# Three empty buffers in SBUF: the normed stream, the second operand and the arena start 192 bytes further on against the weights

## The chip, the cores and the metric

The kernel runs on one core of a Trainium2 chip. The metric is the device time of one execution in microseconds (us); the median of three runs before the change is 3683.33 us.

## The reference

The model is two stacks of two layers each over 512 tokens of width 1024, in float32. The first stack also carries 256 context tokens. Every layer is a mixer and a feed-forward part:

```
first stack, layer 0:  mLSTM heads and a 31-tap convolution      h @ w_in ... @ w_out
first stack, layer 1:  attention with 16 heads, 96 wide          h @ w_in, @ w_uq, @ w_ukv ... @ w_out
first stack, each:     x + gate * ((gelu(conv3(g)) * val) @ ffn_w_out),   g, val = h @ ffn_w_in
second stack, each:    z = h @ w_in;  differential attention and three dilated windows
                       merged = gate0 * (oa @ w_a) + gate1 * (ob @ w_b);  x + rms(merged @ w_out)
                       x + rms((silu(g) * u) @ w_down),                   g, u = h @ w_gate_up
h is always a normed (and in the first stack modulated) x
```

Most of the arithmetic is a dense product of a 1024-wide stream with a weight matrix.

## The kernel before

Tokens lie on the free axis and features on the 128 partitions, so a product is computed as weights (stationary, 128x128 blocks) against the stream (moving, 512 columns for the latent tokens and 256 for the context tokens), gathered in a PSUM bank. The weights come from one stream in HBM, in chunks of eight 128x128 blocks. SyncE loads a chunk into `w_raw`, ScalarE rounds it into `w_hi` (line 333), GpSimd writes the rest `w_raw - w_hi` into `w_lo` (line 3542), and TensorE multiplies when both are there. Three such places rotate.

Every float32 product is made of three fp32r matmuls, with both operands split in a high and a low part (lines 283 to 290):

```
for k, ((lh, ll), (rh, rl)) in enumerate(pairs):
    pe.matmul(dst, lh, rh, start=(begin and k == 0), stop=False)
    pe.matmul(dst, lh, rl, start=False, stop=False)
    last = pe.matmul(dst, ll, rh, ...)
```

The profile names the moving operand first and the stationary one second: `pB<-h_lo,w_hi` streams `h_lo` past a block of `w_hi`. TensorE's order is written out by hand; each matmul has its own weight load.

Moving operands are: `h_hi`, `h_lo` (the normed stream, 512 columns a block), `b_hi`, `b_lo` (the second operand: the activations that go into an output matrix), `xh_*` and `xb_*` (the same for the context tokens, 256 columns, in the arena), and, in a part of the feed-forward layers of the second stack, seven half-size products for a pair of chunks (lines 1090 to 1092, 256 columns, 12 matmuls each; Strassen's scheme). These seven take their moving operands, in this order, from `h`; from `xc_t`; from `attP_t` and `attT_t`; from `h`; from `attT_t` for two blocks and `combo_rest`, `attA_t` for two; from `h`; and from `hsum_t`, `arena_t`, `arena_u`. Their weights are halves of `w_hi`, `w_lo` and the pair `w_hi6`, `w_lo6`. In the attention of the second stack the projections of the next heads (line 2840, 512 columns) are put between the small matmuls of scores, transposes and weighted sums. `HOLD` matmuls (line 392) multiply a constant by the identity where TensorE would otherwise have nothing to do.

**Places in the row.** Tensors lie one behind the other in each partition's row, in the order of the program, each start rounded up to 32 bytes. In bytes: `x` 16384, `xc` 8192, `h_hi`, `h_lo`, `b_hi`, `b_lo` 16384 each, `w_raw` 16384, `w_hi` and `w_lo` 12288 each, `w_hi6`, `w_lo6`, `combo_rest` 2048 each, `pc` 1956 (to 1984), `cm` 3584, `mod` 768, `attA`, `attP`, `attT` 6144 each, `hsum` 3072, then 3904 of small tensors, then the arena (53200). Counted modulo 1024 from where `x` starts:

- `xc_t`, `h_*`, `b_*`, `w_raw`, `w_hi`, `w_lo`, `w_hi6`, `w_lo6`, `combo_rest`: remainder 0, as all sizes up to there are whole multiples of 1024
- `attA_t`, `attP_t`, `attT_t`, `hsum_t`: remainder 192, since 1984 + 3584 + 768 = 6336 = 6 x 1024 + 192
- the arena with `xh_*`, `xb_*`, `arena_t`, `arena_u`: remainder 0 again, since 192 + 3904 = 4096

Blocks inside a tensor start at multiples of 512 bytes (stationary) and 1024 or 2048 bytes (moving).

Of the kernel before, what the change touches and what calls it, by code (L numbers as in the profile page):

```python
# [21 lines left out]
P = 128  # L22
# [115 lines left out]
def program(nc, stream, ada, xT, cT, cond, lam, pcol, cmat, trope, brope, bmask, out):  # L138
    with ExitStack() as ctx:
        def sb(name, shape, dt=F32):  # L140
            return ctx.enter_context(nc.sbuf_tensor(name, shape, dt))
# [7 lines left out]
            pass  # L149
        xc = sb("xc", [P, KD, C])  # L150

        with nc.sbuf_tensor("under", [P, 4, KD * T], F32) as under:
            pass
        h_hi, h_lo = sb("h_hi", [P, KD * T], F32R), sb("h_lo", [P, KD * T], F32R)
        b_hi, b_lo = sb("b_hi", [P, KD * T], F32R), sb("b_lo", [P, KD * T], F32R)
        w_raw = sb("w_raw", [P, SLOTS + 1, KD * P])
        w_hi, w_lo = sb("w_hi", [P, SLOTS, KD * P], F32R), sb("w_lo", [P, SLOTS, KD * P], F32R)
        w_hi6, w_lo6 = sb("w_hi6", [P, HALF_K], F32R), sb("w_lo6", [P, HALF_K], F32R)
# [11 lines left out]
        cond_sb = sb("cond_sb", [P, 2 * KD])  # L170
        cond_pad = sb("cond_pad", [P, KD, 32])
        lam_junk = sb("lam_junk", [P, 64])
        with nc.sbuf_tensor("arena", [P, ARENA], F32) as arena:
            pass
        with nc.sbuf_tensor("mla_under", [P, 5376], F32), nc.sbuf_tensor("mla_q", [P, 4, T], F32R) as mla_q, nc.sbuf_tensor("mla_k", [P, 4, TC], F32R) as mla_k:
# [3753 lines left out]
```

## Time and profile before

| what | before |
|---|---|
| median of 3 runs | 3683.33 us (3680.15 to 3687.66) |
| the profiled execution | 3687.39 us, its span 3685.5 us |
| TensorE matmul busy | 3575.2 us (97%), 21374 matmuls |
| VectorE / ScalarE / GpSimd busy | 54% / 44% / 36% |
| granted TensorE clock, mean | 0.993 |
| DMA | 335.87 MB, mean 91 GB/s |

The span is the time from the first to the last instruction of the profiled execution; its own time is 1.9 us longer. The end of a matmul is modelled and overlaps the next one's start, so the pace of TensorE is read from start to start, and a busy share of 97% does not say that the matmuls follow one another as fast as they could.

### The profile page before, as it was taken

How to read it: one execution, taken by the hardware profiler on the slowest of the kernel's cores; microseconds unless marked ns; L12 is line 12 of the kernel's file. 1: busy time of each engine (PE TensorE's matmuls, PEld its weight loads, DVE VectorE, ACT ScalarE, POOL GpSimd, SP SyncE). 2: the span in 40 equal slices, each digit the busy share in tenths (PEclk: the TensorE clock that was granted, in tenths of full speed). 3: DMA queues.
4: the chain of work that ended last, by engine and by line, in shares of the span. 5: the costliest groups of instructions: out<-in, count | busy, mean ns of one | idle time of the engine just before them, and what ended most of it. 6: DMA issues, size and time to landing. Idle time of an engine off the chain costs nothing.

```text
span 3685.5 us, 56698 instructions
## 1 busy us (share of the span) xinstructions
PE 3575.2 (97%) x21374; PEld 2943.5 (80%) x21374; DVE 1996.1 (54%) x3030; ACT 1627.2 (44%) x2837; POOL 1326.6 (36%) x618
## 2 busy tenths in 40 slices
PE   7999999999999999999999999999999999999998
PEld 5875788888877777888777778789977777878997
DVE  4757553333357775343555553657556565356555
ACT  4344432221266663232655542545455554335444
POOL 2530332232331113444422234345542333434555
PEclk9999999999999999999999999999999999999999
DMA  5368321111220002322311222222322222222332
GB/s 210 118 210 306 106 77 63 63 63 63 69 80 24 24 24 92 103 92 97 102 58 63 70 75 97 73 100 87 115 89 71 65 70 69 86 92 75 109 103 92
DMA packets 85384, 335.87 MB, mean 91 GB/s; under 512 B 9648, under 2 KB 9776, under 8 KB 78640
## 3 DMA queue, kind: packets, MB, share of 16 engines
q1 hardware_dynamic: 84448, 330.79, 27.0%
q8 instruction: 147, 2.41, 0.3%
q10 hardware_dynamic: 720, 2.10, 0.2%
q14 instruction: 69, 0.57, 0.1%
HBM read 329.18 MB, written 2.10 MB: 90 GB/s over the span
## 4 chain that ended last, share of the span: by engine, by line
issue 45%; PE 37%; POOL 14%; DVE 3%; ACT 1%; POOLq 0%; ACTq 0%; DVEq 0%
POOL w_lo L3542 14%; PE pB L287 6%; PE pB L288 6%; PE pB L289 6%; PE pT L1090 2%; PE pT L1091 2%; PE pT L1092 2%; PE pT L289 1%; PE pT L288 1%; PE pT L287 1%; PE pO L287 1%; PE pO L1090 1%; PE pO L1092 1%; PE pO L1091 1%; PE pO L288 1%
## 5 line engine op out<-in xcount | busy, mean ns | idle before, releaser
L3542 POOL TENSOR_TENSOR w_lo<-w_raw,w_hi 128x1024 fp32r<-128x1024 f32 x448 | 1095.7, 2448 | 2075.2 <-ACT w_hi L333 2074.1
L333 ACT ACTIVATE w_hi<-w_raw 128x1024 fp32r<-128x1024 f32 x448 | 472.3, 1055 | 568.2 <-PE pB L289 372.6
L287 PE MATMUL pB<-h_hi,w_hi 128*128 128x512 f32 x1508 | 594.8, 394 | 18.6 <-DVE h_lo L477 6.0
L288 PE MATMUL pB<-h_lo,w_hi 128*128 128x512 f32 x1508 | 587.4, 390 | 0.0
L289 PE MATMUL pB<-h_hi,w_lo 128*128 128x512 f32 x1508 | 586.9, 389 | 0.0
L287 PE MATMUL pB<-b_hi,w_hi 128*128 128x512 f32 (+1 forms) x1084 | 400.9, 370 | 7.9 <-POOL w_lo L3542 4.3
L288 PE MATMUL pB<-b_lo,w_hi 128*128 128x512 f32 (+1 forms) x1084 | 396.0, 365 | 0.0
L289 PE MATMUL pB<-b_hi,w_lo 128*128 128x512 f32 (+1 forms) x1084 | 395.6, 365 | 0.0
L287 PEld LDWEIGHTS pB<-h_hi,w_hi 128*128 128x128 f32 x1508 | 283.7, 188 | 93.2 <-issue 15.5
L289 PEld LDWEIGHTS pB<-h_hi,w_lo 128*128 128x128 f32 x1508 | 283.5, 188 | 59.6
L2840 PE MATMUL pB<-h_hi,w_hi 128*128 128x512 f32 x800 | 330.4, 413 | 0.0
L288 PEld LDWEIGHTS pB<-h_lo,w_hi 128*128 128x128 f32 x1508 | 283.8, 188 | 56.6 <-issue 1.2
L2840 PE MATMUL pB<-h_hi,w_lo 128*128 128x512 f32 x800 | 314.6, 393 | 0.0
L2840 PE MATMUL pB<-h_lo,w_hi 128*128 128x512 f32 x800 | 314.0, 393 | 0.0
L1116 POOL TENSOR_TENSOR w_lo<-w_raw,w_hi 128x512 fp32r<-128x512 f32 x144 | 206.6, 1449 | 180.9 <-ACT w_hi L1111 177.1
L287 PEld LDWEIGHTS pB<-b_hi,w_hi 128*128 128x128 f32 x1084 | 205.1, 189 | 45.6 <-POOL w_lo L3542 4.7
L289 PEld LDWEIGHTS pB<-b_hi,w_lo 128*128 128x128 f32 x1084 | 205.2, 189 | 33.1
L288 PEld LDWEIGHTS pB<-b_lo,w_hi 128*128 128x128 f32 x1084 | 205.4, 189 | 32.3 <-issue 1.2
L2840 PEld LDWEIGHTS pB<-h_hi,w_hi 128*128 128x128 f32 x800 | 150.4, 188 | 53.9 <-issue 24.9
L2840 PEld LDWEIGHTS pB<-h_hi,w_lo 128*128 128x128 f32 x800 | 150.3, 188 | 33.6
L2840 PEld LDWEIGHTS pB<-h_lo,w_hi 128*128 128x128 f32 x800 | 150.9, 189 | 31.2 <-issue 5.1
L3051 ACT ACTIVATE attT<-pT 128x256 f32<-128x256 f32 (+1 forms) x64 | 31.5, 492 | 223.5 <-PE pT L2898 223.5
(673 smaller groups left out, 7200.5 us busy)
## 6 DMA issues: line engine op xcount, KB each, us to landing
w_raw<-stream SPq DMA_DIRECT2D x520, 512.0 KB, 3.3
under<-ada SPq DMA_DIRECT2D x42, 1024.0 KB, 5.3
arena<-ada SPq DMA_DIRECT2D x6, 1024.0 KB, 16.8
x<-xT SPq DMA_DIRECT2D x1, 2048.0 KB, 8.1
out<-x SPq DMA_DIRECT2D x8, 256.0 KB, 2.1
xc<-cT SPq DMA_DIRECT2D x1, 1024.0 KB, 26.5
arena<-bmask ACTq DMA_DIRECT2D x1, 1024.0 KB, 4.9
w_hi<-arena SPq DMA_DIRECT2D x4, 192.0 KB, 9.9
```

Of the source, the lines that this page charges most:

```text
L287: pe.matmul(dst, lh, rh, start=(begin and k == 0), stop=False)
L288: pe.matmul(dst, lh, rl, start=False, stop=False)
L289: last = pe.matmul(dst, ll, rh, start=False, stop=(end and k == len(pairs) - 1))
L333: act.activation(w_hi[:, s, :], w_raw[:, s, :], ACT.Copy).then_inc(hi_ready, 1)
L1090: pe.matmul(dst, wh[:, o], hh, start=begin, stop=False, skip_group_check=True)
L1091: pe.matmul(dst, wh[:, o], hl, start=False, stop=False, skip_group_check=True)
L1092: last = pe.matmul(dst, wl[:, o], hh, start=False, stop=(kt == 3), skip_group_check=True)
L1116: pool.tensor_tensor(lo, block_source(n, i), hi.bitcast(F32), ALU.subtract).then_inc(block_lo, 1)
L2840: last = pe.matmul(bank[s][:, :], wl if i % 3 == 2 else wh, hl if i % 3 == 1 else hh, start=(i == 0), stop=(i == CHUNK - 1))
L3051: act.activation(flat(attT)[:, o:o + w], pT[:, 0:w], ACT.Copy).then_inc(pair_ca, 1)
L3542: pool.tensor_tensor(w_lo[:, s, :], w_raw[:, s, :], w_hi[:, s, :].bitcast(F32), ALU.subtract).then_inc(lo_ready, 1)
```

## The change

Three buffers that nothing reads or writes are allocated. The first (192 bytes) stands in front of `h_hi`, the second (832 bytes) behind `b_lo`, the third (192 bytes) in front of the arena. `under`, which names the room of `h` and `b` under another type, and all the names laid over the arena start behind the buffers too. No instruction is added, removed or reordered.

```diff
@@ -149,10 +149,12 @@
         xc = sb("xc", [P, KD, C])
 
+        sb("place_h", [P, 48])
         with nc.sbuf_tensor("under", [P, 4, KD * T], F32) as under:
             pass
         h_hi, h_lo = sb("h_hi", [P, KD * T], F32R), sb("h_lo", [P, KD * T], F32R)
         b_hi, b_lo = sb("b_hi", [P, KD * T], F32R), sb("b_lo", [P, KD * T], F32R)
+        sb("place_w", [P, 208])
         w_raw = sb("w_raw", [P, SLOTS + 1, KD * P])
@@ -170,6 +172,7 @@
         lam_junk = sb("lam_junk", [P, 64])
+        sb("place_arena", [P, 48])
         with nc.sbuf_tensor("arena", [P, ARENA], F32) as arena:
             pass
```

Modulo 1024, `h_*` and `b_*` go from 0 to 192, and so does the arena (1024 + 192 bytes further on). Everything from `w_raw` to the small tensors moves by 192 + 832 = 1024 bytes and keeps its remainder: the weights, `combo_rest` 0, the `att` strips and `hsum` 192. `x` and `xc` do not move.

## Rows read from the trace of the kernel before

**Rows 1.** The page, busy time and granted clock in 40 slices

```profile
PE 3575.2 (97%) x21374; PEld 2943.5 (80%) x21374; DVE 1996.1 (54%) x3030; ACT 1627.2 (44%) x2837; POOL 1326.6 (36%) x618
...
PEclk9999999999999999999999999999999999999999
```

**Rows 2.** Waits of TensorE, longest: us in total, times, longest

```profile
PE pS L491 <- ACT attT L356: 17.0, 1, 17.0
```

**Rows 3.** Timeline of TensorE, feed-forward chunks: start, length

```profile
1500.24 0.39 PE L287 MATMUL pB<-h_hi,w_hi 128*128 128x512 f32 x1
...
1505.68 0.39 PE L287 MATMUL pB<-h_hi,w_hi 128*128 128x512 f32 x1
```

**Rows 4.** Timeline of TensorE in a pair of half-size products

```profile
2520.49 0.28 PE L1090 MATMUL pT<-h_hi,w_hi 128*128 128x256 f32 x1
...
2521.93 0.28 PE L1090 MATMUL pO<-xc_t,w_hi 128*128 128x256 f32 x1
...
2523.37 0.29 PE L1090 MATMUL pT<-attP_t,w_hi 128*128 128x256 f32 x1
...
2523.84 0.28 PE L1091 MATMUL pT<-attP_t,w_hi 128*128 128x256 f32 x1
...
2524.75 0.28 PE L1090 MATMUL pO<-h_hi,w_hi 128*128 128x256 f32 x1
...
2526.17 0.29 PE L1090 MATMUL pT<-attT_t,w_hi 128*128 128x256 f32 x1
...
2527.58 0.28 PE L1090 MATMUL pB<-h_hi,w_hi 128*128 128x256 f32 x1
...
2530.43 0.28 PE L1090 MATMUL pT<-h_hi,w_hi 128*128 128x256 f32 x1
```

**Rows 5.** Line 1090: duration in ns, min/median/max, first and last start

```profile
L1090 PE MATMUL pT<-h_hi,w_hi x144: 277/283/283, 2417.4 to 3628.0; 128*128 128x256 f32 x144
...
L1090 PE MATMUL pT<-attP_t,w_hi x144: 276/277/554, 2423.3 to 3630.9; 128*128 128x256 f32 x144
```

**Rows 6.** Timeline: matmuls and the weight loads beside them

```profile
1003.98 0.39 PE L287 MATMUL pB<-b_hi,w_hi 128*128 128x512 f32 x1
1003.98 0.19 PEld L288 LDWEIGHTS pB<-b_lo,w_hi 128*128 128x128 f32 x1
...
1004.66 0.28 PE L287 MATMUL pT<-xb_hi,w_hi 128*128 128x256 f32 x1
1004.66 0.19 PEld L288 LDWEIGHTS pT<-xb_lo,w_hi 128*128 128x128 f32 x1
```

**Rows 7.** Timeline: a row of HOLD matmuls

```profile
1022.36 3.19 PE L392 MATMUL pT<-cm 128*128 128x256 f32 x14
```

**Rows 8.** Groups by line and form, 512 columns: busy us, mean ns

```profile
L287 PE MATMUL pB<-h_hi,w_hi 128*128 128x512 f32 x1500 | 592.2, 395 | 18.6 <-DVE h_lo L477 6.0 <-DVE h_lo L2737 5.8 <-POOL w_lo L3542 5.2
...
L2840 PE MATMUL pB<-h_hi,w_hi 128*128 128x512 f32 x800 | 330.4, 413 | 0.0
L287 PE MATMUL pB<-b_hi,w_hi 128*128 128x512 f32 x828 | 325.6, 393 | 7.9 <-POOL w_lo L3542 4.3 <-DVE b_lo L1299 1.6 <-DVE under L2485 1.0
...
L287 PE MATMUL pO<-b_hi,w_hi 128*128 128x512 f32 x92 | 37.1, 403 | 1.4 <-DVE under L2485 1.0 <-issue 0.3 <-ACT attA L2382 0.2
```

**Rows 9.** The same groups, 256 columns

```profile
L287 PE MATMUL pB<-b_hi,w_hi 128*128 128x256 f32 x256 | 75.3, 294 | 0.0
...
L287 PE MATMUL pT<-xh_hi,w_hi 128*128 128x256 f32 x240 | 67.8, 282 | 0.0
...
L287 PE MATMUL pO<-xh_hi,w_hi 128*128 128x256 f32 x112 | 31.6, 282 | 0.0
...
L287 PE MATMUL pT<-xb_hi,w_hi 128*128 128x256 f32 x110 | 31.1, 282 | 0.0
...
L287 PE MATMUL pO<-xb_hi,w_hi 128*128 128x256 f32 x66 | 18.6, 282 | 0.0
```

**Rows 10.** The same groups, a matmul of an arena tensor against a strip

```profile
L2920 PE MATMUL pO<-arena,attT 128*128 128x128 f32 x256 | 33.7, 275 | 0.0
```

## The prediction

> **What bounds the kernel now.** The page comes first: TensorE is busy for 97% of the span, no other engine for more than 54%, and the granted clock is full in all 40 slices, its 2.4 GHz level [rows 1]. The list of TensorE's waits comes second, and its longest is one wait of 17.0 us in 3685.5 [rows 2]. So the time is nearly the sum of the distances from one matmul's start to the next, and anything that shortens these distances everywhere shortens the kernel. The timeline shows what they are. In a feed-forward chunk with 512 columns, 24 matmuls start between 1500.24 and 1505.68 us, which is 5.44 / 24 = 226.7 ns each [rows 3]. 512 columns at 2.4 GHz take 213.3 ns, so 13.4 ns of each matmul are not columns. With 256 columns of `h`, 12 matmuls take 2521.93 - 2520.49 = 1.44 us, or 120.0 ns each, against 106.7 ns of columns: 13.3 ns over [rows 4]. The surcharge is the same for both widths, hence one per matmul, and it is no wait.
>
> **Does it hang on places in the row?** The change touches nothing else, so this is the question, and the trace before has an experiment in it. The seven half-size products of a pair are the same instruction with the same kind of weights; only the tensor that is streamed differs. Product 0 streams `h` (remainder 0 modulo 1024, as the weights have) at 120.0 ns, product 1 streams `xc_t` (remainder 0) at 2523.37 - 2521.93 = 1.44 us for 12, again 120.0. Product 2 streams `attP_t` and `attT_t`, remainder 192. Its first four matmuls still take 2523.84 - 2523.37 = 0.47 us, then eight take 2524.75 - 2523.84 = 0.91 us: 113.75 ns each. Product 3 is back on `h` and takes 2526.17 - 2524.75 = 1.42 us, or 118.3 [rows 4]. The median duration of all 144 such matmuls says the same for every one of the 36 pairs (144 / 4): 283 ns from `h`, 277 ns from `attP_t`, both into `pT` [rows 5]. So a moving operand that lies 192 bytes off the weights modulo 1024 costs 6.25 ns less once the stream of matmuls has settled, and settling takes about four of them.
>
> It fits a collision between two reads of TensorE: the load of the next weights begins in the same 10 ns as the matmul, for 512 and for 256 columns alike [rows 6]. The two reads then start from the same remainder before the change and 192 bytes apart after it. As the load stands beside the first part of the matmul in both widths, and as the surcharge is equal in both, I take the saving of 6.25 ns for 512 columns too. That is the one step that no row shows directly. The bounds for it: nothing (a surcharge of 13.4 ns that has another cause), and down to the HOLD matmuls, 14 of which fill 3.19 us of busy time [rows 7]. They are 256 columns of plain float32, but their distance is that of 512 columns: if the last one is as long as a 512-column one, 0.39 us [rows 3], then 2.80 us are left for 13 distances, 215.4 ns. From 226.7 to 215.4 would be 11.3 ns.
>
> Here the Trainium skill speaks against the change. "SBUF — State Buffer", section "Who interferes with whom", gives TensorE two read ports, one for the moving operand and one for the weight load, independent of each other, and says that it never waits on anyone; its section on operand start alignment asks only for a start at a multiple of the element size, and says that this is legality and not speed. By this rule all seven products would run at one pace and the change would be worth nothing (3683 us). The trace does not agree: 120.0 against 113.75 ns for one instruction.
>
> **The sum.** Four groups gain and one loses.
> 1. 512 columns, plain chunks: 1500 of `h`, 828 and 92 of `b` on line 287 [rows 8], each of them three times (lines 288 and 289 have the same counts): 2420 x 3 = 7260 matmuls x 6.25 ns = 45.4 us. Bounds 0 and 7260 x 11.3 = 82.0 us.
> 2. 512 columns between the attention's matmuls, line 2840: 800 x 3 = 2400 [rows 8]. Their mean is 413 ns where the plain ones have 395: the stream is broken off time and again by other matmuls, and settling takes four. In full it would be 15.0 us; I take two thirds, 10.0. Bounds 0 and 27.1.
> 3. 256 columns, plain: 256 of `b`, 240 + 112 of `xh`, 110 + 66 of `xb` [rows 9], 784 x 3 = 2352 x 6.25 ns = 14.7 us. This is what product 2 shows directly.
> 4. The 36 pairs. One takes 2530.43 - 2520.49 = 9.94 us now [rows 4]. Afterwards products 0, 3, 5 and 6 stream from remainder 192 throughout, 12 x 113.75 ns = 1.365 us each. Product 1 (`xc_t`, stays at 0) now comes behind a settled stream at 192, as product 3 comes behind one of the other kind today, so I give it that one's 1.42. Products 2 and 4 keep their 1.38 and 2527.58 - 2526.17 = 1.41 us, for product 2 still follows `xc_t` and half of product 4 still mixes `combo_rest` (0) with `attA_t` (192). In all 4 x 1.365 + 1.42 + 1.38 + 1.41 = 9.67, a gain of 0.27 us a pair, 9.7 us in 36.
> 5. The arena goes onto the remainder of the `att` strips. Where one is streamed past the other as weights (256 matmuls on line 2920 [rows 10]) the two now meet: at most 256 x 6.25 ns = 1.6 us, which I charge in full.
>
> Nothing is added on any engine's queue, and no transfer gets longer by a row of the trace. A faster TensorE asks for weights sooner, but GpSimd, the last in their chain, is busy for 36% and ScalarE for 44% [rows 1], so a pace 2.8% higher is covered. Sum: 45.4 + 10.0 + 14.7 + 9.7 - 1.6 = 78.2 us. Against the profiled execution that is a span of 3685.5 - 78.2 = 3607.3 us and a time of 3687.39 - 78.2 = 3609.2; the median of the runs stands 4.1 us below that execution, so the prediction is 3683.3 - 78.2 = 3605 us, 2.1% faster.
>
> **The rivals.** For each, 0.2% (7 us) is what a measurement of this kernel can tell from no change.
> - **The wide matmuls gain less.** A 512-column matmul goes on for 113 ns after the point at which a 256-column one has ended, with the load already done; its reads could make up what they lost. Then items 1 and 2 give between a tenth and a half, 5 to 28 us instead of 55, and the time is 3632 to 3655 us. Against it stands the equal surcharge of 13.4 and 13.3 ns. With none of it left the time would be 3683.3 - 22.8 = 3660.5. Together 13 in 100.
> - **Place means nothing.** Product 2 is faster for another reason, such as what the other engines do at that moment of each pair, since the trace has its products always in the same order. Then the time is 3683, within 0.2%. For it: after product 2 the pace of product 3 (118.3 ns) is not at once the old one, though its operand lies at 0. Against it: product 4, half `attT_t` and half a mix with `combo_rest`, takes 1.41 us [rows 4], between 1.365 and 1.44 as its share of remainder 192 asks, and it comes at another moment of the pair than product 2. 6 in 100.
> - **A wide matmul collides later.** It reads 2048 bytes and passes remainders that a narrow one doesn't reach within its weight load. Shifted by 192 bytes, the collision could move from the load's beginning to a place where it costs more. At the same size with the other sign, 9660 x 6.25 = 60 us lost against 22.8 gained, the time is 3683.3 + 37.6 = 3721 us. It decides as soon as the wide distance passes 226.7 + 22.8 / 9.66 = 229.1 ns. Speaking for it: right after a switch from `xc_t`, four matmuls take 0.47 us, 117.5 ns, so a switch is no gain at once. Against: the settled part shows no such place. 5 in 100.
> - The forecast itself: 76 in 100.
>
> **How the numbers follow.** The likeliest case alone spans 3590 to 3625 us: item 1 from 5 to 8 ns a matmul, item 2 between its bounds. Downwards the floor of the HOLD matmuls gives (82.0 - 45.4) + (27.1 - 10.0) = 54 us more, 3551 us; I end the range at 3585, since product 2 stops well short of its own floor. Upwards it takes in most of the first rival, to 3645. Outside lie about 2 in 10. Faster by over 0.2%: the forecast and the first rival, 0.89; within 0.2% 0.06; slower 0.05.
>
> **What would show it.** In the timeline of the changed kernel a run of 24 matmuls from `h` with 512 columns takes 5.29 us instead of 5.44 (220.4 ns a step), the modelled durations fall from 389 or so to about 383 ns, and product 0 takes 1.365 us. Product 1 is the one that stays near 1.42 to 1.44. The counts, the other engines' busy times and the DMA volume are unchanged, and no new wait of TensorE of more than a few us appears. The prediction is wrong in its main step if the wide distance stays within 2 ns of 226.7, and wrong as a whole if product 0 stays at 1.44 us.

## The result, and the profile after

The changed kernel takes 3711.91 us (median of four runs, 3710.78 to 3719.19) against 3682.07 before (median of four runs too): a ratio of 1.0077, with a 95% interval from 1.0065 to 1.0089. It is slower by 0.8%, where 3605 us had been predicted. The profiled execution takes 3719.19 us with a span of 3717.3, 31.8 us more than before.

The page of the changed kernel answers to [rows 1]: the counts are the same, the other engines are as busy as before within 3 us, and TensorE is busy for 29.8 us more.

```profile
PE 3605.0 (97%) x21374; PEld 2924.4 (79%) x21374; DVE 1996.5 (54%) x3030; ACT 1624.5 (44%) x2837; POOL 1328.9 (36%) x618
...
PEclk9999999999999999999999999999999999999999
```

The waits of TensorE hardly differ: it is idle for 3717.3 - 3605.0 = 112.3 us, 2.0 more than before. The longest wait, which answers to [rows 2], went from 17.0 to 17.4 us, and the two waits for the transfer of `ada` from 5.9 to 8.1:

```profile
PE pS L494 <- ACT attT L359: 17.4, 1, 17.4
PE pB L290 <- POOL w_lo L3545: 8.2, 6, 2.2
PE pB L553 <- DMA under<-ada: 8.1, 2, 6.7
```

and in the kernel before:

```profile
PE pB L550 <- DMA under<-ada: 5.9, 2, 5.5
```

So the time is in the distances from one matmul's start to the next again. The timeline of TensorE in a plain feed-forward chunk answers to [rows 3] (the added lines shift line 287 to 290):

```profile
1512.18 0.39 PE L290 MATMUL pB<-h_hi,w_hi 128*128 128x512 f32 x1
...
1517.78 0.39 PE L290 MATMUL pB<-h_hi,w_hi 128*128 128x512 f32 x1
```

24 matmuls with 512 columns take 5.60 us, 233.3 ns each, where it was 226.7. They were to get 6.25 ns shorter and got 6.6 ns longer. A pair of half-size products, as in [rows 4], went as forecast:

```profile
3419.25 0.28 PE L1093 MATMUL pT<-h_hi,w_hi 128*128 128x256 f32 x1
...
3420.61 0.28 PE L1093 MATMUL pO<-xc_t,w_hi 128*128 128x256 f32 x1
...
3422.03 0.29 PE L1093 MATMUL pT<-attP_t,w_hi 128*128 128x256 f32 x1
...
3423.41 0.28 PE L1093 MATMUL pO<-h_hi,w_hi 128*128 128x256 f32 x1
...
3428.89 0.28 PE L1093 MATMUL pT<-h_hi,w_hi 128*128 128x256 f32 x1
```

Product 0 from `h` takes 3420.61 - 3419.25 = 1.36 us, against a forecast of 1.365 and 1.44 before; product 1 from `xc_t`, whose place is unchanged, 1.42 as forecast; the pair 9.64 us, against a forecast of 9.67 and 9.94 before. The groups by form say it for all matmuls. Their mean durations answer to [rows 8]; each wide one is longer by 3 to 6 ns:

```profile
L290 PE MATMUL pB<-h_hi,w_hi 128*128 128x512 f32 x1500 | 600.1, 400 | 16.8 <-DVE h_lo L480 6.0 <-DVE h_lo L2740 5.8 <-POOL w_lo L3545 3.7
...
L2843 PE MATMUL pB<-h_hi,w_hi 128*128 128x512 f32 x800 | 332.9, 416 | 0.0
L290 PE MATMUL pB<-b_hi,w_hi 128*128 128x512 f32 x828 | 330.1, 399 | 8.2 <-POOL w_lo L3545 4.5 <-DVE b_lo L1302 1.5 <-DVE under L2488 0.9
```

The sum of all distances under 300 ns between starts, by moving tensor, gives the balance against before: 512 columns from `h` +33.8 us and from `b` +16.8; 256 columns from `h` -8.7, from `b` -2.1, from `xh` -2.0, from `xb` -1.6, and from the other operands of the pairs (`xc_t`, `attP_t`, `attT_t`, `arena_t`, `arena_u`, `hsum_t`) -5.4 together. That is +50.6 - 19.8 = 30.8 of the 31.8 us.

### The profile page after: what moved, and what is told of

The parts are those of the page before. It is cut to its first block, busy times and chain, and to the rows that moved or that the text cites. A ratio compares the mean times of both kernels' runs of the same rounds, so it can differ in the third digit from the quotient of the medians.

```text
span 3717.3 us, 56698 instructions
## 1 busy us (share of the span) xinstructions
PE 3605.0 (97%) x21374; PEld 2924.4 (79%) x21374; DVE 1996.5 (54%) x3030; ACT 1624.5 (44%) x2837; POOL 1328.9 (36%) x618
## 3 DMA queue, kind: packets, MB, share of 16 engines
q1 hardware_dynamic: 84448, 330.79, 26.6%
## 4 chain that ended last, share of the span: by engine, by line
issue 45%; PE 36%; POOL 14%; DVE 3%; ACT 2%; POOLq 0%; DMA 0%; ACTq 0%; DVEq 0%; SPq 0%
POOL w_lo L3545 14%; PE pB L290 7%; PE pB L291 6%; PE pB L292 6%; PE pT L1093 2%; PE pT L1094 1%; PE pT L1095 1%; PE pT L292 1%; PE pT L290 1%; PE pT L291 1%; PE pO L290 1%; PE pO L292 1%; PE pO L291 1%; PE pO L1095 1%; PE pO L1093 1%
## 5 line engine op out<-in xcount | busy, mean ns | idle before, releaser
L290 PE MATMUL pB<-h_hi,w_hi 128*128 128x512 f32 x1508 | 602.6, 400 | 16.8 <-DVE h_lo L480 6.0
L291 PE MATMUL pB<-h_lo,w_hi 128*128 128x512 f32 x1508 | 595.8, 395 | 0.0
L292 PE MATMUL pB<-h_hi,w_lo 128*128 128x512 f32 x1508 | 595.6, 395 | 0.0
L2843 PE MATMUL pB<-h_hi,w_hi 128*128 128x512 f32 x800 | 332.9, 416 | 0.0
L2843 PE MATMUL pB<-h_lo,w_hi 128*128 128x512 f32 x800 | 317.1, 396 | 0.0
L2843 PE MATMUL pB<-h_hi,w_lo 128*128 128x512 f32 x800 | 316.9, 396 | 0.0
```

The lines of the kernel that those rows point to most:

```text
L292: last = pe.matmul(dst, ll, rh, start=False, stop=(end and k == len(pairs) - 1))
L2843: last = pe.matmul(bank[s][:, :], wl if i % 3 == 2 else wh, hl if i % 3 == 1 else hh, start=(i == 0), stop=(i == CHUNK - 1))
```

## The experiments

Below, the distance of a tensor is the mean of its distances under 300 ns in the whole kernel. In the runs of TensorE alone the settled distance of a case is the mean of its last 35 distances.

After the result the theory was this. **Theory A:** what counts is where the streamed operand starts against the weights; 192 bytes between them make a 256-column matmul shorter and a 512-column one longer. The rivals: the loss comes from the arena (B), the place of the moving operand alone counts (C), other engines make the difference (D).

**The arena alone.**

```diff
         lam_junk = sb("lam_junk", [P, 64])
+        sb("place_arena", [P, 48])
```

> Only the 192 bytes in front of the arena: xh, xb, arena_t and arena_u go to remainder 192, h, b and the weights stay at 0. Theory A (what counts is how far the moving operand lies from the weights, and 192 bytes help a 256-column matmul and hurt a 512-column one): the 512-column distance stays 226.7 ns, the context matmuls (1584 with 256 columns) gain 2 to 6 ns each, product 6 some, in all 4 to 10 us faster than before, about 3675. Theory B (the loss of the whole change comes from somewhere else than the wide matmuls, for instance from the arena meeting the att strips): this kernel alone is slower than before by a good part of the 30 us.

Measured: 3675.41 us against 3685.32 for the kernel before on the same chip, ratio 0.9977 (0.9966 to 0.9987). The distance of 512 columns from `h` is 227.9 ns (228.1 before, with the interruptions in it). `xh` goes from 119.7 to 117.8 ns, `xb` from 119.7 to 117.6, `arena_u` from 119.5 to 113.2. Theory B falls: this part of the change is a gain.

**The streams alone.**

```diff
+        sb("place_h", [P, 48])
         with nc.sbuf_tensor("under", [P, 4, KD * T], F32) as under:
...
+        sb("place_w", [P, 208])
         w_raw = sb("w_raw", [P, SLOTS + 1, KD * P])
```

> Only the buffers around h and b, none in front of the arena: h and b at remainder 192, all else at 0. Theory A: 9660 wide matmuls at about 233.5 ns instead of 226.7 lose 60 to 66 us, the 256-column ones of h and b (2100 or so) gain 10 to 13, so 3725 to 3735 us, some us slower than the whole change. Theory B: most of the loss is gone, 3690 us or less.

Measured: 3723.96 us, ratio 1.0108 (1.0091 to 1.0126), 1 us below the expected range, with wide distances of 233.4 ns from both `h` and `b`. The two parts, +1.08% and -0.23%, make the +0.77% of the whole within their intervals.

**Everything shifted by the same 192 bytes.** Only the first buffer, so that `h`, `b`, the weights, the strips and the arena keep their distances from one another.

```diff
+        sb("place_h", [P, 48])
         with nc.sbuf_tensor("under", [P, 4, KD * T], F32) as under:
```

> One buffer of 192 bytes in front of h and nothing else: h, b, the weights, the att strips and the arena all move by 192 bytes and keep their distances from one another. Theory A (the difference between moving operand and weights counts): distances of 226.7 and 120.0 ns as before, time 3682 within 0.2%. Theory C (the place of the moving operand by itself counts): 233.5 and 113.75 ns as in the changed kernel, 3705 to 3720 us.

Measured: 3682.64 us, ratio 0.9993 (0.9983 to 1.0003). Wide distances average 228.1 ns from `h`, and the narrow ones of `xh` 119.7 ns, as before. Only `x` and `xc` stayed where they were: `xc_t` now lies 192 bytes before the weights instead of level with them, and goes from 120.0 to 118.2 ns. The place of the moving operand alone means nothing (C falls).

**TensorE alone, 32 places.**

```diff
+for kt in range(KD):
+    a, b = kt * T + d // 4, kt * P + w // 4
+    hi, lo = hi_all[:, a:a + n], lo_all[:, a:a + n]
+    whi, wlo = wh_all[:, b:b + P], wl_all[:, b:b + P]
+    mm(pe, dst, whi, hi, ...); mm(pe, dst, whi, lo, ...); mm(pe, dst, wlo, hi, ...)
```

> Leaves out the whole model: one float32 input is split into two moving tensors and two stationary ones, and TensorE alone runs 48 matmuls in the kernel's pattern (high-high, low-high, high-low) for each place of the moving operand from 0 to 992 bytes past the weights' remainder in steps of 32, with 512 and with 256 columns, then for 128 to 448 columns at 0 and 192, then with the weights moved by 192. Nothing else uses SBUF meanwhile. Theory A: at 0 bytes 226.7 and 120.0 ns, at 192 bytes 233.5 and 113.75 ns, and with weights and moving operand both moved by 192 the values of 0. Theory D (other engines' reads and writes make the difference, TensorE alone does not): 216 to 227 ns at every place. If the wide matmul collides at a place past the narrow one's end, the surcharge at 192 bytes jumps from about 7 to about 20 ns between 256 and 512 columns while that at 0 bytes stays near 13.

The timeline shows the first matmul of each case of 48. Lines 15 to 46 are the places 0, 32, 64 and so on of the moving operand; on lines 47 and 48 the weights stand at 192 and the moving operand at 0 and 192. A case at a width other than 512 and 256 stands on line 15 (place 0) or 21 (place 192).

```profile
31.87 0.40 PE L16 MATMUL acc_t<-hi_t,whi_t 128*128 128x512 f32 x1
...
43.08 0.40 PE L17 MATMUL acc_t<-hi_t,whi_t 128*128 128x512 f32 x1
...
54.07 0.40 PE L18 MATMUL acc_t<-hi_t,whi_t 128*128 128x512 f32 x1
...
87.72 0.39 PE L21 MATMUL acc_t<-hi_t,whi_t 128*128 128x512 f32 x1
...
98.92 0.40 PE L22 MATMUL acc_t<-hi_t,whi_t 128*128 128x512 f32 x1
...
110.11 0.40 PE L23 MATMUL acc_t<-hi_t,whi_t 128*128 128x512 f32 x1
...
120.99 0.40 PE L24 MATMUL acc_t<-hi_t,whi_t 128*128 128x512 f32 x1
...
570.32 0.33 PE L15 MATMUL acc_t<-hi_t,whi_t 128*128 128x320 f32 x1
...
577.37 0.34 PE L15 MATMUL acc_t<-hi_t,whi_t 128*128 128x384 f32 x1
...
585.70 0.36 PE L15 MATMUL acc_t<-hi_t,whi_t 128*128 128x448 f32 x1
...
595.61 0.22 PE L21 MATMUL acc_t<-hi_t,whi_t 128*128 128x128 f32 x1
...
606.31 0.33 PE L21 MATMUL acc_t<-hi_t,whi_t 128*128 128x320 f32 x1
...
613.37 0.34 PE L21 MATMUL acc_t<-hi_t,whi_t 128*128 128x384 f32 x1
...
621.69 0.36 PE L21 MATMUL acc_t<-hi_t,whi_t 128*128 128x448 f32 x1
...
631.40 0.39 PE L47 MATMUL acc_t<-hi_t,whi_t 128*128 128x512 f32 x1
```

Divided by 48: at 32 bytes 233.4 ns, at 64 229.0, at 192 (line 21) 233.3, at 256 (line 23) 226.7. Apart from the very first case, whose first distances are 427 ns, cases 256 bytes apart have the same average within 0.2 ns, so the map repeats every 256 bytes, and 0 is its best of eight places for 512 columns. The settled distances in ns:

| bytes | 0 | 32 | 64 | 96 | 128 | 160 | 192 | 224 |
|---|---|---|---|---|---|---|---|---|
| 512 columns | 226.7 | 233.3 | 228.8 | 233.4 | 233.5 | 234.3 | 233.4 | 233.4 |
| 256 columns | 120.0 | 117.8 | 117.7 | 120.1 | 118.7 | 118.7 | 117.7 | 118.3 |

With weights and moving operand both at 192 the settled distance of 512 columns is 226.7 again. With 256 columns at 192, 113.75 ns had been expected and 117.7 came; the 113.3 of the pairs appears once, on line 47. With nothing else running, the wide values of a plain chunk at 0 and at 192 are reproduced to 0.1 ns. Theory D falls for them.

The widths test the rival of the prediction that forecast a loss; it let the wide matmul pass places that a narrow one doesn't reach. A 256-column block is 1024 bytes long and passes the 256-byte pattern four times, so it meets every place of the pattern. Nor does the loss set in at a width and stay: for 320 columns it is 147 ns at either place ((577.37 - 570.32) / 48 and (613.37 - 606.31) / 48), for 384 columns 173 at either, for 448 columns 206.5 at 0 against 202.3 at 192, the other way round. The next run, `bench_causes`, has three widths more, each after a pause. From 320 to 384 columns the distance grows by 26.6 ns, which is 64 columns at 2.4 GHz, one a cycle; what is left over these columns' time is the surcharge of the prediction (settled values, ns):

| columns | 256 | 320 | 384 | 448 | 480 | 496 | 504 | 512 |
|---|---|---|---|---|---|---|---|---|
| distance at 0 | 120.0 | 146.7 | 173.3 | 206.7 | 216.5 | 223.4 | 226.7 | 226.7 |
| surcharge at 0 | 13.3 | 13.4 | 13.3 | 20.0 | 16.5 | 16.7 | 16.7 | 13.4 |
| distance at 192 | 113.3 or 117.7 | 146.7 | 173.3 | 202.3 | 216.0 | 226.7 | 228.8 | 233.4 |
| surcharge at 192 | 6.6 or 11.0 | 13.4 | 13.3 | 15.6 | 16.0 | 20.0 | 18.8 | 20.1 |

So which of the two places is better hangs on the width, and even at place 0 the surcharge is not one amount per matmul: that 256 and 512 columns have the same one there does not hold for the widths between them.

**What meets what.** 48 matmuls for each case, most after a pause, among them:

```diff
+    # columns, moving offset, more for lo, stationary offset, more for lo, stationary columns, gap before
...
+    (512, 192, 0, 0, 0, 128, 0),
+    (256, 192, 0, 0, 0, 128, 0),
+    (512, 0, 0, 0, 0, 128, 0),
+    (256, 192, 0, 0, 0, 128, 0),
...
+    (512, 0, 0, 0, 0, 32, 1),
+    (512, 192, 0, 0, 0, 32, 1),
```

> Leaves out the whole model, as bench did: 48 matmuls of TensorE alone per case, most cases after a pause. Open: why 256 columns at 192 bytes settle at 113.3 ns in the pairs but at 117.7 in bench, and what meets what. Theory A1 (moving stream against weight load, in four places of 64 bytes that repeat every 256 bytes): the surcharge at 0 and 192 bytes falls when the stationary block has 96, 64 or 32 columns instead of 128, since the load is shorter; adding 1024 bytes to the low parts changes nothing; the state that 256 columns settle in hangs on what ran before, so after a pause or after other widths 192 bytes give sometimes 113.3 and sometimes 117.7. Theory A2 (address bits above 256 count too): 113.3 against 117.7 follows the 1024 bytes added to one of the parts, whatever ran before. Theory E (the surcharge is a fixed cost of a matmul and not of the load): 64 or 32 stationary columns keep 13.4 and 20 ns. Offsets of 4 to 24 bytes with 512 columns: about 233 ns, one line more to read than at 0.

Lines 18 to 21 are the first four cases of that list; lines 51 to 56 have 96, 64 and 32 stationary columns at 0 and at 192; those with 96 and 32 are shown, from the 13th to the 37th matmul. Two weight loads stand beside them, of 128 and of 32 columns:

```profile
48.39 0.40 PE L18 MATMUL acc_t<-hi_t,whi_t 128*128 128x512 f32 x1
...
59.59 0.28 PE L19 MATMUL acc_t<-hi_t,whi_t 128*128 128x256 f32 x1
...
65.05 0.39 PE L20 MATMUL acc_t<-hi_t,whi_t 128*128 128x512 f32 x1
...
69.83 0.19 PEld L20 LDWEIGHTS acc_t<-lo_t,whi_t 128*128 128x128 f32 x1
...
75.94 0.28 PE L21 MATMUL acc_t<-hi_t,whi_t 128*128 128x256 f32 x1
...
81.59 0.28 PE L22 MATMUL acc_t<-hi_t,whi_t 128*128 128x256 f32 x1
...
340.94 0.39 PE L51 MATMUL acc_t<-hi_t,whi_t 128*96 128x512 f32 x1
...
346.46 0.39 PE L51 MATMUL acc_t<-hi_t,whi_t 128*96 128x512 f32 x1
...
352.93 0.40 PE L52 MATMUL acc_t<-hi_t,whi_t 128*96 128x512 f32 x1
...
358.41 0.39 PE L52 MATMUL acc_t<-hi_t,whi_t 128*96 128x512 f32 x1
...
388.84 0.40 PE L55 MATMUL acc_t<-hi_t,whi_t 128*32 128x512 f32 x1
...
394.40 0.40 PE L55 MATMUL acc_t<-hi_t,whi_t 128*32 128x512 f32 x1
394.40 0.11 PEld L55 LDWEIGHTS acc_t<-lo_t,whi_t 128*32 128x32 f32 x1
...
400.87 0.39 PE L56 MATMUL acc_t<-hi_t,whi_t 128*32 128x512 f32 x1
...
406.43 0.39 PE L56 MATMUL acc_t<-hi_t,whi_t 128*32 128x512 f32 x1
```

The same case, 256 columns at 192, takes 5.46 us for 48 (line 19) when wide matmuls at 192 ran before it, and 5.65 (line 21) when wide ones at 0 did: 113.3 or 117.7 ns once settled, and it stays there for the rest of its 48. After a pause it is 113.3, and after 256 columns at 0 (line 23) 113.3 too. The slower state does not need wide matmuls before it: in `bench` the narrow case at 192 came behind a narrow one at 160 and settled at 117.7. Nor does a pause always wipe out what ran before: 256 columns at 64 after a pause settle at 117.8 here, and at 113.3 in `bench_mixed` below. Adding 1024 bytes to one part or another changed no settled distance by more than 0.1 ns, so A2 (address bits above 256 bytes count) falls and the history decides.

The load's length is answered by lines 51 to 56. A weight load lasts 188 ns with 128 stationary columns, and 161, 135 and 108 ns with 96, 64 and 32. With 96 stationary columns the distance is 5.52 / 24 = 230.0 ns at 0 and 5.48 / 24 = 228.3 at 192; with 64 it is 230.0 and 231.1; with 32 it is 5.56 / 24 = 231.7 at both. A load of 108 ns instead of 188 does not lower the surcharge at 0, against A1 (stream against load), but raises it from 13.4 to 18.4; the rival E, a surcharge that keeps its 13.4 and 20 ns, falls as well. The influence of the place goes from 6.6 ns with 128 stationary columns to none with 32, for this width. Moving the operand by 4 to 24 bytes gave 231.6 to 237.8 ns, by -16 236.6 and by -4 230.7, all longer than at 0.

**The map put to the test on the whole kernel: 256 and 64 bytes.**

```diff
+        sb("place_h", [P, 64])
...
+        sb("place_w", [P, 192])
```

This is streams_256; streams_64 has 16 and 240 in place of 64 and 192.

> h and b 256 bytes further on instead of 192, the weights 1024 bytes, the arena 1024. Theory A with the period of 256 bytes that bench showed: distances 226.7 and 120.0 ns, time as before within 0.2%, though every tensor behind x has moved. If a move by itself, or any remainder other than 0 modulo 1024, did the harm: 3710 to 3725 us.

Measured: 3685.76 us, ratio 1.0001 (0.9991 to 1.0010). Moving everything behind `xc` costs nothing when the places against one another stay the same modulo 256.

> h and b 64 bytes further on, the weights and the arena 1024. By bench's distances (228.8 ns for 512 columns, 117.7 for 256) 9660 wide matmuls lose 2.1 ns each, 20 us, and some 2100 narrow ones gain 2.3 ns each, 5 us: about 3697 us, half as slow as at 192 bytes. If only alignment to 64 bytes mattered: no change. If any remainder but 0 costs the same: 3715 to 3725.

Measured: 3703.80 us against 3686.33, ratio 1.0051 (1.0034 to 1.0067), 17.5 us of loss for an expected 15 net. The wide distances average 230.1 ns from `h` and 230.8 from `b`, 2.0 and 3.6 more than before; with other matmuls in between they come less near to the bench's 2.1.

**Mixtures of places.** The low moving part, the high moving part and the low weights each at 0, 64, 128 or 192 bytes against the high weights.

```diff
+    # columns, moving offset, more for lo, stationary offset, more for lo, stationary columns, gap before
+    (512, 0, 0, 0, 0, 128, 1),
+    (512, 0, 0, 0, 64, 128, 1),
...
+    (512, 64, 64, 0, 128, 128, 1),
...
+    (256, 0, 0, 0, 0, 64, 1),
+    (256, 192, 0, 0, 0, 64, 1),
```

> Leaves out the whole model, TensorE alone as in the other benches, each case after a pause: the place of the high moving part, of the low moving part and of the low stationary part each at 0, 64, 128 and 192 bytes against the high stationary part, 64 combinations, with 512 and with 256 columns, then 256 columns with 96, 64 and 32 stationary ones. Theory A3 (a matmul's stream meets the load of the next weights, so its distance is set by that pair of places): with 512 columns only combinations in which all three neighbours agree at 0 give 226.7, each pair that differs adds a third of what all three add, and no mixture goes below. If some mixture lets the stream and the load take turns all the way, it shows here as less than 226.7 (down to 220 would be worth 60 us of the kernel). Theory E2 (the surcharge is a fixed 13 ns, to which places only add): nothing below 226.7 with 512 columns.

The timeline of the two shortest with 512 columns, from the 13th to the 37th matmul: all at 0 (line 14), and 64 / 128 / 128 (line 40, the places of the high moving, the low moving and the low weight part). Lines 144 and 145 have 256 columns and 64 stationary ones, at 0 and at 192.

```profile
25.77 0.39 PE L14 MATMUL acc_t<-hi_t,whi_t 128*128 128x512 f32 x1
...
31.22 0.39 PE L14 MATMUL acc_t<-hi_t,whi_t 128*128 128x512 f32 x1
...
340.40 0.39 PE L40 MATMUL acc_t<-hi_t,whi_t 128*128 128x512 f32 x1
...
345.87 0.39 PE L40 MATMUL acc_t<-hi_t,whi_t 128*128 128x512 f32 x1
...
1238.19 0.28 PE L144 MATMUL acc_t<-hi_t,whi_t 128*64 128x256 f32 x1
...
1240.91 0.28 PE L144 MATMUL acc_t<-hi_t,whi_t 128*64 128x256 f32 x1
...
1244.62 0.28 PE L145 MATMUL acc_t<-hi_t,whi_t 128*64 128x256 f32 x1
...
1247.48 0.28 PE L145 MATMUL acc_t<-hi_t,whi_t 128*64 128x256 f32 x1
```

5.45 / 24 is 227 ns and 5.47 / 24 is 228; over their last 35 distances they average 226.8 and 227.7, and the other 62 lie between 228.7 and 235.7. None of the 64 beats the 226.7 ns of the kernel before. The thirds don't add up as expected (0 / 0 / 64 gives 231.0 though two of three neighbours are unmoved), so that part of A3 is wrong. With 256 columns the best is 113.3, for both moving parts at 64 or 192 with the low weights at 0, or at 192 with 128. With fewer stationary columns the narrow distances at 0 and 192 are 116.0 and 117.1 for 96, 2.72 / 24 = 113.3 and 2.86 / 24 = 119.2 for 64, and 117.8 and 116.7 for 32. So with 64 stationary columns the two places have changed roles, and for a narrow matmul a short load does not make the place harmless.

**A version built on the map.** Wide operands at 0, narrow ones at 192.

```diff
         x = sb("x", [P, KD, T])
+        sb("place_xc", [P, 48])
...
         xc = sb("xc", [P, KD, C])
 
+        sb("place_h", [P, 208])
...
+        sb("place_combo", [P, 48])
         combo_rest = sb("combo_rest", [P, HALF_K], F32R)
+        sb("place_pc", [P, 208])
...
+        sb("place_arena", [P, 48])
```

> A version built on the map: h and b, which are streamed with 512 columns, stay at 0; everything that is streamed with 256 columns alone goes to 192 (the arena, xc_t, combo_rest; the att strips are there already). Theory A with settled states: the 8 to 10 us of the arena alone, and in the 36 pairs product 1 from 120.0 to between 113.5 and 118 ns (1 to 3 us) and the combo_rest half of product 4 from 118 to 114 or so (0.5 us); in all 3672 to 3676 against 3685, faster than before by 0.25 to 0.35%. If the whole gain of the arena came from something else than its matmuls, nothing is added to it: 3676 or more.

Measured: 3672.99 us against 3684.87, ratio 0.9965 (0.9951 to 0.9979), the lowest median of all these kernels. The interval overlaps that of the arena alone (0.9966 to 0.9987), so by the times the further step is not shown; by the distances it is. `xc_t` goes from 120.0 to 114.9 ns, `combo_rest` from 117.9 to 113.4, `attA_t` from 118.6 to 113.2, the rest as with the arena alone.

## Why the prediction was wrong

The step that failed is this one: "As the load stands beside the first part of the matmul in both widths, and as the surcharge is equal in both, I take the saving of 6.25 ns for 512 columns too." Equal surcharges at one place did not carry over to another. At 0 they are 13.4 and 13.3 ns; at 192 they are 20.0 for 512 columns and 6.6 (in the pairs) or 11.0 for 256. The likeness at 0 was a coincidence of two widths: 448 columns have 20.0 there. The step before it, "hence one per matmul", fails by the same rows.

- **What bounds the kernel** was read rightly: TensorE's distances made the whole difference, and no wait did.
- **Items 1 and 2** were to give 55.4 us and cost 50.6 instead, which is 106 us; forecast and result lie 107 us apart, and the errors of the other items nearly cancel. The lower bound of their cost was set at nothing, and the trace before had no row of a wide matmul at another place that would have excluded a loss.
- **Item 3**, the plain narrow ones, was to give 14.7 us and gave 5.7. The saving was taken from the pairs, where matmuls with 256 columns follow one another. Here they follow wide ones in groups of 24. `xh` settled at 117.8 ns, not 113.75. In `bench_causes` this second state follows wide matmuls at 0, in `bench` narrow ones at 160. Why `xh` has it in the changed kernel, where the wide ones stand at 192 too, was not settled, but its trace shows that the group before decides there as well: 16 groups of `xb` behind 24 wide matmuls settle at 117.8, 8 groups behind 18 wide ones at 113.3, and 192 matmuls of `b` behind 120 of `h` at 113.3.
- **Item 4**, the pairs, was right in cause and size: 0.30 us a pair instead of 0.27, 10.8 us by the pair shown. The distances of the pairs' operands in the whole kernel gained 14.1 (8.7 and 5.4 above), but some 3.4 of these (37 x 93 ns) have nothing to do with the place. In the profile before, 37 matmuls of the pairs stand 210 to 219 ns apart just after waits, where the granted clock was at its 1.2 GHz level; in the profile after there are none. The line gives a stretch of it; the 0.50 behind the busy times is the granted clock:

```profile
2423.00:2428.00 5.00, 4.66 (x22) 4.69 (x23) 4.90 (x5) 2.89 (x7) 5.00 (x4) 0.50 0.27 77
```

- **Item 5** was charged 1.6 us. The 256 matmuls of the arena against the strips take 26.0 us of distance against 25.9: nothing.
- **The rivals.** The one with 5 in 100, a loss of the same size with the other sign, gave 3721 us, and it stood above its deciding distance of 229.1 ns with 233.3. As it was put, its mechanism was wrong all the same: since the pattern repeats after 256 bytes, there is no place that only the wide matmul passes. That a wide matmul loses something late in its stream for another reason is not excluded; its surcharge at 192 grows from 13.4 ns with 320 columns to 20 with 496 and 512. "Place means nothing" is excluded: a shift of everything by 192 bytes is free, and the same shift of the streams alone costs 1.08%.

What stays open: what within TensorE makes the surcharge at all, why with 512 columns a short load makes the place harmless and leaves the surcharge, and what the two settled states of narrow matmuls are made of. The collision of the two reads was a guess; no run here shows it. The runs show that the wide distances need no other engine, and that they hang on the place of the moving operand against the weights modulo 256 bytes, on the two widths, and, for narrow matmuls, on what ran before.

## What to carry to other kernels

When a saving is read from one shape of an instruction, it holds for that shape. If the time is mostly made of another, measure that one alone before the layout is changed: a bench of TensorE by itself gave the distances of 32 places in one run, and those of the kernel's plain chunks at 0 and 192 to 0.1 ns. Place narrow and wide moving operands separately, and keep the wide ones of 512 float32r columns, with 128 stationary ones, at the weights' remainder modulo 256 bytes.

## What the runs showed of the hardware that was not expected

- The place of a float32r matmul's moving operand in the row, against the weights, changes its pace: 226.7 ns at 0, 229 at 64 and 233 to 234 at the other six multiples of 32 below 256, with 512 columns and nothing else running. The Trainium skill says in "SBUF — State Buffer", section "Who interferes with whom", that TensorE never waits on anyone; no other engine has part in this, so these numbers don't speak against it, but its pace still changes with where its own two operands lie against each other.
- Where all distances of a case are alike to the nanosecond, they are whole multiples of 6.67 ns, a quarter of the 26.6 ns that 64 columns more took: 113.3 is 17 of them, 120.0 is 18, 146.7 is 22, 173.3 is 26, 206.7 is 31, 226.7 is 34. Other places do not simply add a step. At 192 the wide distances in `bench` alternate between about 231 and 236 ns, and averages such as 117.7, 202.3 and 228.8 are no multiples.
- The pace has a memory. The same 48 matmuls ran at 113.3 or at 117.7 ns depending only on the matmuls before them.
- A weight load of fewer columns is shorter (188, 161, 135 and 108 ns for 128, 96, 64 and 32), and 512-column matmuls with the short load follow one another no faster: 231.7 ns with 32 stationary columns, 226.7 with 128.
